# Down tiles by halves of the channels, two first tiles interleaved, zero products and moved sums in a two-layer decoder trunk

## The chip, the core and the metric

The kernel is one program on one core of a Trainium2 chip. The metric is the device time of one execution in microseconds (us): the median of several runs. TensorE is the engine for matrix products (PE, and PEld for its weight loads), VectorE (DVE) and ScalarE (ACT) do the elementwise work, SyncE (SP) issues most transfers.

## What is computed

Two decoder layers over 256 tokens of 1024 channels, all in float32:

```python
for i in range(DEPTH):
    mod = c_act @ w_mod[i] + b_mod[i]
    sh1, sc1, g1, sh2, sc2, g2 = jnp.split(mod, N_MOD, axis=-1)
    h = modulate(rmsnorm(x, norm1_g[i]), sh1, sc1)
    y = short_conv_mixer(...) if i % 2 == 0 else pool_mixer(...)
    x = x + g1[:, None, :] * y
    h = modulate(rmsnorm(x, norm2_g[i]), sh2, sc2)
    x = x + g2[:, None, :] * peer_ffn(h, ...)
return rmsnorm(x, final_g)
```

`peer_ffn` projects `h` to queries, scores them against two sets of 128 keys, picks 16 of 16384 experts for each head and token, and sums `gate * gelu(h . u_expert) * v_expert`. The kernel computes it densely: all experts' products with `u` ("up"), the gates scattered into a dense matrix, and the product with `v` ("down").

## The kernel before, in words

**Tiles.** Every weight matrix is cut into tiles of 128 x 1024. They pass through a ring of 4 slots in one order for the whole program: `conv_in` (24 tiles), `conv_out` (8), `query` (16), `up` (128), `down` (128) in layer 0, then `pool_in` (8), `pool_group` (4), `pool_out` (8), `query`, `up` and `down` again in layer 1. For each tile SyncE loads `raw[s]`, ScalarE rounds it into `high[s]` (L371), VectorE forms the rest `low[s]` (L557, called through `slot`, which works 3 tiles ahead of TensorE), and TensorE multiplies. Each product is made of three: `high` by `mov_h`, `high` by `mov_l`, `low` by `mov_h`, where `mov_h` and `mov_l` are the rounded activations and their rest. The counter `product` goes up by one for each finished tile and frees its slot.

**Projection tiles** (L1093, functions `three` and `project`) are 8 channels x 3 products of 256 columns, into one of the two banks of `ps`. The next tile but one needs the bank emptied (`evac_dve` or `evac_act`).

**Down tiles** (L1242, `down_tile`) are the experts' rows: for each of four banks of `acc` (two halves of the tokens times two halves of the channels; banks 0 and 1 hold the first half of the channels) three products of 512 columns. All 128 tiles add up in the same four banks. Behind the last tile ScalarE (banks 0 and 2, L540) and VectorE (1 and 3, L1026) copy them to `E`; TensorE turns `E` back channel by channel with products by the unit matrix (L1271, eight for each half), `turned_back(c)` lying in `ps` for channels 0 to 3 and in `acc` for 4 to 7; VectorE adds each channel, scaled, to `X` (L1032) and counts `x_ready`.

**Norms.** ScalarE squares each channel of `X` (L400), TensorE adds the squares of each token by products with one column of ones (L1064, two for each channel), ScalarE takes the root (L404), VectorE the reciprocal and a diagonal (L607, L610), TensorE spreads it over the partitions (`spread`, L1080), VectorE scales each channel (`scaled`, L629), ScalarE shifts and rounds it to `mov_h` (L417), VectorE forms `mov_l` (`rest`, L635). In `norm`, `scaled` and `rest` take turns with a lag of two channels. The first tile behind a norm waits for `mov_l` channel by channel (`moving`). There are five norms: 0 and 1 in layer 0, 2 and 3 in layer 1, and the last one, 4. Norms 1 and 3 get their squares already added over the channels (`total`, L683), so that TensorE has only two products there.

**Modulation.** The products of `c` and `w_mod` are formed on VectorE (L576) into `macc`; TensorE adds them over the partitions with products of one column (`sum_mod`, L1053, 8 for each of six parts). For layer 1 parts 0 and 1 are summed right before the last down tile of layer 0. The rows of the experts picked are turned by six products with the unit matrix (L1213, once in each layer).

The order on each engine is that of its program. The engines are tied by semaphores alone.

## Time and profile before

| | |
|---|---|
| median of 3 runs | 1914.95 us (1914.13 to 1916.62) |
| the profiled execution | 1915.88 us, of which 1914.1 us from its first to its last instruction |
| TensorE busy | 1864.7 us (97% of the span) |
| VectorE busy | 1525.1 us (80%) |
| ScalarE busy | 860.3 us (45%) |
| mean granted clock of TensorE | 0.985 of full speed |

The times of single steps below come from that one execution. A busy share of 97% says that nearly all of the time is dense products; the rest sits where TensorE waits or runs at the lower of its two clock levels (1.2 instead of 2.4 GHz, granted clock 0.50). A row's idle time names what ended the wait.

### The profile page before, as it was taken

What the parts mean: (1) busy time and instruction counts of PE and PEld (TensorE: products, weight loads), DVE (VectorE), ACT (ScalarE), POOL (GpSimd) and SP (SyncE); (2) the same over time, 40 slices, a digit from 0 to 9 for tenths busy, and PEclk for the clock granted to TensorE, in tenths of its full rate; (3) what the DMA queues carried; (4) which work ended last, traced back from release to release, by engine and by line L of the source; (5) the groups of instructions that cost most, each with busy time, mean ns of one, the idle gap of its engine ahead of it and who ended that gap; (6) DMA issues with size and microseconds to landing.
All of it is one profiled execution on the core that took longest, in us unless ns stands there. A gap on an engine that the chain in (4) does not pass through costs nothing.

```text
span 1914.1 us, 39829 instructions
## 1 busy us (share of the span) xinstructions
PE 1864.7 (97%) x14820; PEld 1729.5 (90%) x14820; DVE 1525.1 (80%) x2634; ACT 860.3 (45%) x1281; POOL 4.0 (0%) x8
## 2 busy tenths in 40 slices
PE   5989999999999999999999999999999999999998
PEld 5989999999999888888889899999999988888887
DVE  7986698888888888788868668889788888885554
ACT  3334444454334444454544544444433444444543
POOL 0000000000000000000000000000000000000000
PEclk9998999999999999999989999999999999999998
DMA  7976455555454555698835655555445455555552
GB/s 298 333 280 227 145 185 179 185 169 167 159 159 142 170 175 170 235 333 318 316 112 168 243 168 172 183 186 180 164 151 163 138 172 164 174 194 191 191 192 88
DMA packets 101339, 370.38 MB, mean 194 GB/s; under 512 B 11168, under 2 KB 11552, under 8 KB 100640
## 3 DMA queue, kind: packets, MB, share of 16 engines
q1 hardware_dynamic: 100848, 367.43, 57.0%
q10 hardware_dynamic: 432, 2.23, 0.3%
q8 instruction: 29, 0.48, 0.1%
q14 instruction: 30, 0.25, 0.0%
HBM read 366.47 MB, written 3.15 MB: 193 GB/s over the span
## 4 chain that ended last, share of the span: by engine, by line
PE 91%; DVE 6%; DMA 2%; issue 1%; ACT 1%; SPq 0%; DVEq 0%; ACTq 0%
PE ps L1093 46%; PE acc L1242 37%; PE gp L1191 5%; DVE acts L576 2%; DVE low L557 1%; PE gp L1053 1%; PE gp L1180 1%; DMA raw<-conv_in 1%; DMA acts<-w_mod 1%; PE gp L1064 0%; DVE acts L629 0%; DMA raw<-conv_out 0%; DVE acts L934 0%; ACT high L371 0%; PE gp L1080 0%
## 5 line engine op out<-in xcount | busy, mean ns | idle before, releaser
L557 DVE TENSOR_TENSOR low<-raw,high 128x1024 fp32r<-128x1024 f32 x596 | 727.6, 1222 | 325.9 <-ACT high L371 323.6
L371 ACT ACTIVATE high<-raw 128x1024 fp32r<-128x1024 f32 x593 | 626.9, 1057 | 483.4 <-PE acc L1242 384.8
L1093 PE MATMUL ps<-mov_h,high 128*128 128x256 f32 x2704 | 778.8, 288 | 15.2 <-DVE mov_l L635 7.2
L1093 PE MATMUL ps<-mov_l,high 128*128 128x256 f32 x2704 | 770.3, 285 | 0.0
L1093 PE MATMUL ps<-mov_h,low 128*128 128x256 f32 x2704 | 770.0, 285 | 0.0
L1093 PEld LDWEIGHTS ps<-mov_h,high 128*128 128x128 f32 x2704 | 523.7, 194 | 18.7 <-issue 13.9
L1093 PEld LDWEIGHTS ps<-mov_l,high 128*128 128x128 f32 x2704 | 524.8, 194 | 0.0
L1093 PEld LDWEIGHTS ps<-mov_h,low 128*128 128x128 f32 x2704 | 524.2, 194 | 0.0
L1242 PE MATMUL acc<-high,mov_h 128*128 128x512 f32 x1024 | 403.4, 394 | 1.0 <-DVE mov_l L991 0.8
L1242 PE MATMUL acc<-high,mov_l 128*128 128x512 f32 x1024 | 399.6, 390 | 0.0
L1242 PE MATMUL acc<-low,mov_h 128*128 128x512 f32 x1024 | 399.5, 390 | 0.0
L482 ACT ACTIVATE acts<-ps 128x256 f32 (+1 forms) x256 | 98.5, 385 | 433.6 <-PE ps L1093 433.6
L1242 PEld LDWEIGHTS acc<-high,mov_h 128*128 128x128 f32 x1024 | 192.8, 188 | 41.2 <-DVE mov_l L991 2.2
L1242 PEld LDWEIGHTS acc<-high,mov_l 128*128 128x128 f32 x1024 | 192.8, 188 | 40.9
L1242 PEld LDWEIGHTS acc<-low,mov_h 128*128 128x128 f32 x1024 | 193.0, 188 | 39.2
L861 DVE TENSOR_TENSOR hot<-hot,gate 128x1536 bf16<-128x1536 bf16 x128 | 121.9, 952 | 0.0
L576 DVE SCALAR_TENSOR_TENSOR acts<-acts,cact 128x1024 f32<-128x1024 f32 x86 | 110.1, 1280 | 5.8 <-DMA acts<-w_mod 5.4
L991 DVE TENSOR_TENSOR mov_l<-acts,mov_h 128x256 fp32r<-128x256 f32 x256 | 106.5, 419 | 2.7 <-ACT mov_h L514 2.7
L1191 PEld LDWEIGHTS gp<-hot 128*128 128x128 bf16 x3072 | 96.4, 97 | 9.7 <-issue 8.4
L1191 PE MATMUL gp<-hot 128*128 128x64 bf16 x3072 | 104.1, 193 | 0.0
L514 ACT ACTIVATE mov_h<-acts 128x256 fp32r (+1 forms) x256 | 101.4, 399 | 0.0
L857 DVE TENSOR_TENSOR hot<-sm,idx 128x1024 bf16<-128x1024 bf16 x128 | 87.7, 685 | 0.0
(108 smaller groups left out, 743.1 us busy)
## 6 DMA issues: line engine op xcount, KB each, us to landing
raw<-up SPq DMA_DIRECT2D x256, 512.0 KB, 3.3
raw<-down SPq DMA_DIRECT2D x256, 512.0 KB, 3.9
acts<-w_mod SPq DMA_DIRECT2D x84, 512.0 KB, 5.3
raw<-query SPq DMA_DIRECT2D x32, 512.0 KB, 3.5
raw<-conv_in SPq DMA_DIRECT2D x24, 512.0 KB, 6.9
acts<-w_mod SPq DMA_DIRECT2D x6, 1024.0 KB, 15.4
raw<-conv_out SPq DMA_DIRECT2D x8, 512.0 KB, 7.3
raw<-pool_in SPq DMA_DIRECT2D x8, 512.0 KB, 4.4
```

The source lines that it names most:

```text
L371: nc.scalar.activation(flat(high[s]), tile_row(s), ACT.Copy).then_inc(high_ready, 1)
L482: nc.scalar.activation(A[:, bass.ds(i * (RING * T) + (first + s) * T, T)], ps[:, s % 2, 0:T], ACT.Gelu).then_inc(evac_act, 1)
L514: nc.scalar.activation(mov_h[:, s], A[:, bass.ds(g * T, T)] if not isinstance(g, int) else A[:, g * T:(g + 1) * T], ACT.Copy).then_inc(wh_ ...
L557: nc.vector.tensor_tensor(flat(low[n % RING]), tile_row(n % RING), flat(high[n % RING]).bitcast(F32), ALU.subtract).then_inc(low_ready, 1)
L576: return nc.vector.scalar_tensor_tensor(macc[:, m], tile, c, macc[:, m], ALU.mult, ALU.add)
L857: nc.vector.tensor_tensor(hot2[:, u], number(0, P), over(idx2, P), ALU.is_equal)
L861: nc.vector.tensor_tensor(hot1[:, u].rearrange("p h n e two -> p (h n) e two"), eq.unsqueeze(2).broadcast_to([P, PAIRS, PARTS, HALF, 2]).r ...
L991: nc.vector.tensor_tensor(mov_l[:, s], A[:, g * T:(g + 1) * T], mov_h[:, s].bitcast(F32), ALU.subtract).then_inc(wl_ready, 1)
L1053: ins = nc.tensor.matmul(gp[:, 1, m * DC + c:m * DC + c + 1], macc[:, m, c * P:(c + 1) * P], ones[:, 0:1], start=True, stop=True)
L1093: ins = nc.tensor.matmul(dst, w[s][:, c], m[:, mv], start=(first and n == 0), stop=(last and n == 2), skip_group_check=skip)
L1191: ins = nc.tensor.matmul(gp[:, u, j * HALF:(j + 1) * HALF], hot2[:, u, j // 2, :, j % 2], hot1[:, u, j // 2, n, :, j % 2], start=(n == 0), ...
L1242: ins = nc.tensor.matmul(acc[:, b, :], w[:, s, tok], flat(v[s])[:, cols], start=False, stop=(closing and n == 2), skip_group_check=True)
```

## The change

1. **Down by halves.** The last four down tiles of each layer are multiplied for banks 0 and 1 first, all four, then for banks 2 and 3. Between the second halves of the first and the second of them stand the turning back of channels 0 to 3, so that the copies, the additions to `X` and the squares of that half can run beside products. The sums of squares of channels 0 and 1 stand before the turning back of channels 4 to 7. ScalarE and VectorE follow the same order, and the high and low parts of the next layer's first three tiles stand between them.
2. **Two tiles side by side.** `first_two` takes the place of the first two tiles of `pool_in` and of both `query` runs: all products by `mov_h` of both tiles channel by channel, then those by `mov_l`. In `norm`, all eight `scaled` stand before the eight `rest` for norms 1 to 3.
3. **Zeros.** `keep_warm` multiplies 128 x 128 zeros, 12 times before `spread` of norms 1 to 4 and 13 times behind it for norms 1 to 3, into `acc[:, 3]`.
4. **Sums moved.** The two modulation sums of layer 1 stand behind the third and the fourth tile of the second last group of four down tiles, 8 products each; VectorE takes them up behind its last additions to `X`.
5. Turning uses the transpose form of the product instead of a plain product with the unit matrix, 22 of them in each layer.
6. The first four tiles of each loop of projection tiles are written out instead of being the loop's first turn.

```diff
@@ -528,17 +529,31 @@
                     last = n0 + first + HALF - RING
                     if half == 1:
                         load_table(ACT.Sqrt)
-                    for s in range(RING):
-                        if last + s + AHEAD < TILES:
+                    ahead(0, last, 0)
+                    weight(first + HALF - 1, RING - 1)
+                    if half == 0:
+                        for s in range(1, RING):
                             ahead(0, last, s)
-                        if s + AHEAD < RING:
...
+                def evac(b):
                     act.wait_ge(acc_done, 3 * layer + b + 1)
                     nc.scalar.activation(E[:, b % 2, (b // 2) * 512:(b // 2 + 1) * 512], acc[:, b, :], ACT.Copy
                                          ).then_inc(acc_out_act, 1)
+                def squares(c0):
+                    for c in range(c0, c0 + DC // 2):
+                        act.wait_ge(x_ready, layer * DC + c + 1)
+                        square(c)
+                evac(0)
+                squares(0)
+                if layer == 0:
+                    ahead(0, last, 1)
+                    ahead(0, last, 2)
+                evac(2)
+                if layer == 0:
+                    ahead(0, last, 3)
+                squares(DC // 2)
...
-                lag = 4 if shift_last else 2
-                for c in range(DC):
-                    if shift_last and c == lag:
-                        shift_last()
-                    scaled(c)
-                    if k < 4 and c >= lag:
-                        rest(c - lag)
-                if k < 4:
+                if k == 0:
+                    lag = 4
+                    for c in range(DC):
+                        if c == lag:
+                            shift_last()
+                        scaled(c)
+                        if c >= lag:
+                            rest(c - lag)
                     for c in range(DC - lag, DC):
                         rest(c)
-                if k == 0:
                     for n in range(1, AHEAD):
                         rest_of(n)
+                else:
+                    for c in range(DC):
+                        scaled(c)
+                    if k < 4:
+                        for c in range(DC):
+                            rest(c)
...
-                    dve.wait_ge(x_ready, DC)
-                    finish_mod(1, (0, 1))
...
-                for j in range(HALF):
+                for j in range(HALF - AHEAD):
...
-                for b in (1, 3):
-                    if b == 1:
-                        dve.wait_ge(acc_done, 3 * layer + 2)
-                    else:
-                        dve.wait_ge(product, n0 + KEYS + RING)
+                def evac(b):
                     nc.vector.tensor_copy(E[:, b % 2, (b // 2) * 512:(b // 2 + 1) * 512], acc[:, b, :]
                                           ).then_inc(acc_out_dve, 1)
+                def add_to_x(c0):
+                    for c in range(c0, c0 + DC // 2):
+                        if c % 2 == 0:
+                            dve.wait_ge(back, (layer * DC + c) // 2 + 1)
+                        nc.vector.scalar_tensor_tensor(X[:, c], turned_back(c),
+                                                       mod[:, 5 * DC + c:5 * DC + c + 1], X[:, c],
+                                                       ALU.mult, ALU.add).then_inc(x_ready, 1)
+                dve.wait_ge(acc_done, 3 * layer + 2)
+                evac(1)
                 dve.wait_ge(reloaded, 16 * (layer + 1))
-                for c in range(DC):
-                    if c % 2 == 0:
-                        dve.wait_ge(back, (layer * DC + c) // 2 + 1)
-                    nc.vector.scalar_tensor_tensor(X[:, c], turned_back(c),
-                                                   mod[:, 5 * DC + c:5 * DC + c + 1], X[:, c],
-                                                   ALU.mult, ALU.add).then_inc(x_ready, 1)
+                add_to_x(0)
+                slot(n0 + KEYS - 3)
+                slot(n0 + KEYS - 2)
+                dve.wait_ge(product, n0 + KEYS + RING)
+                evac(3)
+                add_to_x(DC // 2)
+                slot(n0 + KEYS - 1)
+                if layer == 0:
+                    finish_mod(1, (0, 1))
+                dve.wait_ge(x_ready, DC * (layer + 1))
...
+            def keep_warm(n):
+                for _ in range(n):
+                    nc.tensor.matmul(acc[:, 3, 0:P], zeros[:], zeros[:], start=True, stop=True)
...
+            def first_two(layer, name, evac, evac0):
+                pe.wait_ge(low_ready, AT[layer, name] + 2)
+                pe.wait_ge(evac, evac0 + 2)
+                def one(s, w, m, c, first, last):
+                    return nc.tensor.matmul(ps[:, s, 0:T], w[s][:, c], m[:, c], start=first, stop=last)
+                for c in range(DC):
+                    pe.wait_ge(mh_done, moved[0] * DC + c + 1)
+                    for s in range(2):
+                        one(s, high, mov_h, c, c == 0, False)
+                        one(s, low, mov_h, c, False, False)
+                lag = DC // 2
+                for c in range(DC + lag):
+                    if c < DC:
+                        moving(c)
+                        ins = one(0, high, mov_l, c, False, c == DC - 1)
+                        if c == DC - 1:
+                            ins.then_inc(product, 1)
+                    if c >= lag:
+                        ins = one(1, high, mov_l, c - lag, False, c - lag == DC - 1)
+                ins.then_inc(product, 1)
...
+            def run_behind_norm(layer, name, tiles, evac, evac0):
+                first_two(layer, name, evac, evac0)
+                for s in range(2, RING):
+                    project(layer, name, 0, s, evac, evac0)
+                with pe.Fori(0, tiles // RING - 1) as i:
...
                 spread(2 * layer)
+                if layer == 1:
+                    keep_warm(13)
...
-                    run(1, "pool_in", 8, evac_dve, 32)
+                    run_behind_norm(1, "pool_in", 8, evac_dve, 32)
...
+                keep_warm(12)
                 spread(2 * layer + 1)
-                run(layer, "query", 16, evac_act, out_act)
+                keep_warm(13)
+                run_behind_norm(layer, "query", 16, evac_act, out_act)
...
-                        ins = nc.tensor.matmul(dst[:, tc * P:(tc + 1) * P], src[:, tc * P:(tc + 1) * P], eye,
-                                               start=True, stop=True)
+                        ins = nc.tensor.transpose(dst[:, tc * P:(tc + 1) * P], src[:, tc * P:(tc + 1) * P], eye)
...
+                        def next_sum(m):
+                            if layer == 0:
+                                pe.wait_ge(next_used, NEXT + NEXT * (DC - 1) + m + 1)
+                                if m == 0:
+                                    pe.wait_ge(weighted, 2 * SETS)
+                                    pe.wait_ge(mod_taken, sums[0])
+                                    sums[0] += 1
+                                ins = mod_products(m)
+                                if m == 1:
+                                    ins.then_inc(msum_done, 1)
+                        with pe.Fori(0, HALF // RING - 2) as i:
                             for s in range(RING):
-                                down_tile(i, s, False)
+                                down_tile(i, s)
                         for s in range(RING):
-                            if layer == 0 and s == RING - 1:
-                                pe.wait_ge(next_used, NEXT + NEXT * DC)
-                                pe.wait_ge(weighted, 2 * SETS)
-                                sum_mod((0, 1))
-                            down_tile(HALF // RING - 1, s, s == RING - 1)
-                for c in range(DC):
-                    if c % 4 == 0:
-                        pe.wait_ge(acc_out_act, 2 * layer + c // 4 + 1)
-                        pe.wait_ge(acc_out_dve, 2 * layer + c // 4 + 1)
-                    for tc in range(TC):
-                        ins = nc.tensor.matmul(turned_back(c)[:, tc * P:(tc + 1) * P], E[:, tc, c * P:(c + 1) * P],
-                                               eye, start=True, stop=True)
-                    if c % 2:
-                        ins.then_inc(back, 1)
-            square_sums(4)
+                            down_tile(HALF // RING - 2, s)
+                            if s >= 2:
+                                next_sum(s - 2)
+                        for s in range(RING):
+                            arrived(HALF // RING - 1, s)
+                            down_banks(s, (0, 1), s == RING - 1)
+                def turn_back(c0):
+                    pe.wait_ge(acc_out_act, 2 * layer + c0 // 4 + 1)
+                    pe.wait_ge(acc_out_dve, 2 * layer + c0 // 4 + 1)
+                    for c in range(c0, c0 + DC // 2):
+                        for tc in range(TC):
+                            ins = nc.tensor.transpose(turned_back(c)[:, tc * P:(tc + 1) * P],
+                                                      E[:, tc, c * P:(c + 1) * P], eye)
+                        if c % 2:
+                            ins.then_inc(back, 1)
+                for s in range(RING):
+                    down_banks(s, (2, 3), s == RING - 1).then_inc(product, 1)
+                    if s == 0:
+                        turn_back(0)
+                square_sums(2 * layer + 2, 0, 2)
+                turn_back(DC // 2)
+                square_sums(2 * layer + 2, 2, DC)
+                keep_warm(12)
             spread(4)
```

In the rows of the order, a row is one instruction or several of one kind, with its line, operation, output and inputs, size, and what it waits for.

TensorE from the last down product of layer 0 to the sums of squares, before:

```order
L1242 MATMUL acc<-high,mov_l 128x512
L1271 MATMUL ps<-sm,acts 128x128 [waits acc_out_dve,acc_out_act]
L1271 MATMUL ps<-sm,acts 128x128 x7
L1271 MATMUL acc<-sm,acts 128x128 [waits acc_out_dve,acc_out_act]
L1271 MATMUL acc<-sm,acts 128x128 x7
L1064 MATMUL gp<-ones,acts 128x1 [waits sq_done,weighted]
```

and of the changed kernel, from its last down product on:

```order
L1315 MATMUL acc<-high,mov_l 128x512
L1099 MATMUL gp<-ones,acts 128x1 [waits sq_done]
L1099 MATMUL gp<-ones,acts 128x1
L1099 MATMUL gp<-ones,acts 128x1 [waits sq_done]
L1099 MATMUL gp<-ones,acts 128x1
L1366 MATMUL acc<-sm,acts 128x128 [waits acc_out_dve,acc_out_act]
L1366 MATMUL acc<-sm,acts 128x128 x7
```

Only the second eight turns are left behind the last down product; the first eight now stand 18 down products earlier, and two channels' sums come before the wait for the copies of banks 2 and 3.

VectorE at the same place (the copies of `acc`, the additions to `X`, the low parts of `pool_in`), before:

```order
L557 TENSOR_TENSOR low<-raw,high 128x1024 [waits high_ready] x3
L1026 COPY acts<-acc 128x512 [waits acc_done]
L1026 COPY acts<-acc 128x512 [waits product]
L1032 SCALAR_TENSOR_TENSOR acts<-ps,mod,acts 128x256 [waits back,reloaded]
```

and now:

```order
L1040 COPY acts<-acc 128x512 [waits acc_done]
L1047 SCALAR_TENSOR_TENSOR acts<-ps,mod,acts 128x256 [waits back,reloaded]
L1047 SCALAR_TENSOR_TENSOR acts<-ps,mod,acts 128x256
L1047 SCALAR_TENSOR_TENSOR acts<-ps,mod,acts 128x256 [waits back]
L1047 SCALAR_TENSOR_TENSOR acts<-ps,mod,acts 128x256
L572 TENSOR_TENSOR low<-raw,high 128x1024 [waits high_ready] x2
L1040 COPY acts<-acc 128x512 [waits product]
```

The three low parts (L557, now L572) have moved from before both copies to behind them, two of them ahead of the copy of bank 3.

TensorE around the spreading of norm 2 (`gp<-acts,ones`), before:

```order
L1064 MATMUL gp<-ones,acts 128x1
L1080 MATMUL gp<-acts,ones 128x128 [waits diag_done] x2
L1109 UNCONDITIONAL_BRANCH [waits evac_act]
L1109 ISA
L1101 REGISTER_ALU [waits low_ready]
L1093 MATMUL ps<-mov_h,high 128x256 [waits ml_done,evac_dve]
L1093 MATMUL ps<-mov_l,high 128x256
```

and now:

```order
L1099 MATMUL gp<-ones,acts 128x1
L1094 MATMUL acc<-zeros 128x128 x12
L1119 MATMUL gp<-acts,ones 128x128 [waits diag_done] x2
L1094 MATMUL acc<-zeros 128x128 x13
L1135 MATMUL ps<-mov_h,high 128x256 [waits evac_dve,mh_done,low_ready,evac_act]
L1135 MATMUL ps<-mov_h,low 128x256
L1135 MATMUL ps<-mov_h,high 128x256
L1135 MATMUL ps<-mov_h,low 128x256
```

The first product behind the norm no longer waits for `mov_l` (`ml_done`), and 25 products with zeros stand around the spreading.

## Rows read from the trace of the kernel before

**Rows 1.** The page: the chain that ended last, shares of the span by engine.

```profile
PE 91%; DVE 6%; DMA 2%; issue 1%; ACT 1%; SPq 0%; DVEq 0%; ACTq 0%
```

**Rows 2.** The same chain in time: start us, us, what.

```profile
151.69 51.82 PE ps L1093 x408
...
204.41 1.68 PE gp L1053 x16
...
232.56 201.59 PE ps L1093 x1680
...
434.15 1.34 PE gp L1213 x12
...
977.18 4.46 PE gp L1053 x32
...
981.64 5.06 PE acc L1242 x12
...
990.27 3.97 PE gp L1064 x32
...
1070.20 51.67 PE ps L1093 x408
...
1723.80 174.38 PE acc L1242 x768
...
1901.75 4.08 PE gp L1064 x32
```

**Rows 3.** Stretches: length, busy us (instructions) of each engine, granted clock, DMA.

```profile
147.00:156.50 9.50, 6.63 (x26) 5.99 (x27) 7.11 (x20) 4.96 (x10) 0.00 (x0) 0.50 0.20 80
...
977.00:979.40 2.40, 2.40 (x24) 2.38 (x22) 1.04 (x1) 1.06 (x1) 0.00 (x0) 1.00 0.56 186
979.50:986.10 6.60, 6.60 (x22) 5.63 (x22) 0.78 (x2) 0.97 (x2) 0.00 (x0) 0.50 0.26 101
986.50:993.00 6.50, 6.50 (x60) 6.46 (x58) 4.39 (x11) 3.24 (x8) 0.00 (x0) 1.00 0.01 4
993.20:1003.20 10.00, 7.13 (x29) 6.48 (x30) 7.25 (x21) 5.06 (x10) 0.00 (x0) 0.50 0.00 0
...
1064.50:1068.00 3.50, 1.07 (x9) 0.96 (x8) 1.63 (x6) 0.68 (x2) 0.00 (x0) 1.00 1.00 356
1068.30:1074.90 6.60, 4.70 (x19) 4.43 (x20) 6.39 (x16) 4.60 (x9) 0.00 (x0) 0.50 0.21 87
...
1904.50:1914.00 9.50, 2.54 (x11) 2.15 (x10) 3.87 (x11) 0.26 (x1) 0.00 (x0) 0.50 0.32 110
```

**Rows 4.** Timeline of VectorE behind the layer boundary: start us, us, instructions, idle before.

```profile
978.36 1.23 DVE L557 TENSOR_TENSOR low<-raw,high 128x1024 fp32r<-128x1024 f32 x1 [1.49 <-ACT high L371]
...
996.50 1.26 DVE L629 SCALAR_TENSOR_TENSOR acts<-acts,gs,gp 128x256 f32<-128x256 f32 x3 [1.12 <-PE gp L1080]
...
1006.91 0.42 DVE L926 COPY acts<-ps 128x256 f32<-128x256 f32 x1 [0.56 <-PE ps L1093]
```

**Rows 5.** Timeline of ScalarE at the same place.

```profile
988.21 3.42 ACT L400 ACTIVATE acts<-acts 128x256 f32<-128x256 f32 x8 [1.89 <-DVE acts L1032]
...
997.08 1.31 ACT L417 ACTIVATE mov_h<-acts,mod 128x256 fp32r<-128x256 f32 x3 [2.56 <-DVE acts L629]
```

**Rows 6.** Timeline of TensorE at the same place.

```profile
995.16 1.22 PE L1080 MATMUL gp<-acts,ones 128*128 128x128 f32 x4 [0.94 <-DVE acts L610]
998.31 0.55 PE L1093 MATMUL ps<-mov_h,high 128*128 128x256 f32 x1 [1.92 <-DVE mov_l L635]
```

**Rows 7.** Timeline of TensorE before the second norm of layer 1.

```profile
1067.56 0.71 PE L1080 MATMUL gp<-acts,ones 128*128 128x128 f32 x4 [0.88 <-DVE acts L610]
```

**Rows 8.** Timeline of TensorE: zero products before the first down tile.

```profile
603.90 1.07 PE L1231 MATMUL acc<-zeros 128*128 128x128 bf16 x16
```

**Rows 9.** Timeline of VectorE at the end of layer 1.

```profile
1898.21 0.69 DVE L1026 COPY acts<-acc 128x512 f32<-128x512 f32 x1 [0.67 <-PE acc L1242]
1899.17 1.70 DVE L1032 SCALAR_TENSOR_TENSOR acts<-ps,mod,acts 128x256 f32<-128x256 f32 x4 [0.27 <-PE ps L1271]
```

89 lines of the change are left out of this document (47 added, 42 removed).

## Prediction, made before the changed kernel ran

> **What bounds the kernel now.** The chain that ended last comes first: 91% of it is TensorE [rows 1], and read in time it is nearly all dense stretches, so elementwise work moved beside them costs nothing. The products stay the same in number; a gain must come from the gaps, from the low clock, or from cheaper small products. I then read the stretches around each gap, for busy time and granted clock, and the timelines inside them for who waits for whom. The unit prices are: a projection tile is 201.59 / 70 = 2.88 us; a down tile 174.38 / 64 = 2.72, half of one 1.36 [rows 2]. Five places are left: the norm before `query` in either layer, the layer boundary, the end, and the turning of the rows picked.
>
> **The clock.** It stands at 2.4 GHz (1.00) in dense work and at 1.2 GHz (0.50) for 9.5 us from 147.0, 6.6 from 979.5, 10 from 993.2, 6.6 from 1068.3 and from 1904.5 to the end [rows 3]. Before each fall TensorE had full-width products, then only one-column products or idled: it fell 2.3 us after the sums began at 977.2, and some 2.8 us after the sums began at 990.3 [rows 2, 3]. Before 1068 it had idled since about 1064.4, 3.8 us. I take 3.1 us from the last full product to the fall. It came back 4.9 us (998.31 to 1003.2) and 4.7 us (1070.2 to 1074.9) after full products resumed [rows 2, 3, 6]; I take 4.9. A single run of eight one-column sums of 1.68 us between tiles never brought it down [rows 2].
>
> **Norm before `query`, layer 0.** Nothing ahead of the fall at about 146.6 changes. Before, the first tile waits for VectorE, which takes two steps of 0.40 us a channel (`scaled`, `rest`), and starts 1.81 us behind the first `scaled` (996.50 to 998.31 in the like norm [rows 4, 6]). Here the stretch from 151.69 holds 17 tiles [rows 2]: 16 at 2.88 leave 5.8 us for the first, so the second ends at 160.4. Now only `mov_h` is waited for, in steps of 0.40 (three in 1.31 us, the first 0.58 behind `scaled` [rows 4, 5]), so TensorE starts 1.2 us behind it. At the high clock it needs 4 x 0.12 = 0.48 a channel, ends `mov_h` at 5.0, then 16 `mov_l` products; VectorE ends its 16 steps at 6.4, which holds the last, and both tiles are done 7.2 us behind the first `scaled`, against 10.4. The gain would be 3.2. The zeros: 16 take 1.07 us, so 0.057 each at the high clock, and I take twice that at the low [rows 8]. Twelve last 0.7 or 1.3 us, where the wait for the diagonal is 0.9 [rows 6]; at the low clock they push the spread back 0.35. But TensorE then has full-width products from 147.6, so the clock returns at 152.5, 1 us into the first two tiles, and the rest is held by `mov_l` anyway. With 0.35 and some 0.7 of this lost I take **2.1** (0.7 if zeros do nothing for the clock, 3.5 if it never falls).
>
> **Norm before `query`, layer 1.** The zeros start at 1066.7, before the fall at 1068.2; the clock would be back at 1071.6 instead of 1075.0, and twelve at the high clock fit. First product at 1070.2, 17 tiles in 51.67 [rows 2], second tile done at 1078.7. Now 7.2 to 7.8 behind the first `scaled` at 1068.4, and a wait of ScalarE for the bank, some 0.2. **2.4** (1.0 to 3.1).
>
> **Turning the rows picked.** Six plain products took 1.34 us, 0.22 each [rows 2], on the chain in each layer. No row shows the transpose form. Bounds: 0.22, no change, and 0.057, what a single pass of 128 columns takes [rows 8]. I take 0.11, since one of the 8 sums of 1.68 us also costs two passes of 0.105 that only the weight load can fill [rows 2]. 2 x 6 x 0.11 = **1.3** (0 to 2.0).
>
> **Layer boundary.** Before, the sums at 977.18 take 4.46 us, and the last tile 5.06, because the clock fell in them [rows 2, 3]. Split, each is 1.68 and the tiles 2.72. From 966.1 (the start of the fourth last but one tile, four tiles ahead of 977): sum 1.68, tile 2.72, sum 1.68, so the last group starts at 972.2; the first halves end at 977.6, one second half at 979.0, the turning (0.9) at 979.9, three second halves at 984.0. The first copies (0.69 [rows 9]), four additions (1.70 [rows 9]) and four squares (3.42 / 2 [rows 5]) fit beside that: free, and their cover is 4.1 us of products. Not free: ScalarE's squares put the roundings of `pool_in` late, VectorE stands behind them with two low parts of 1.23 [rows 4] and copies bank 3 at 985.4 instead of 984.2. So that queue costs 1.2 us, of which two channels' sums fill 0.8. Copy 0.7, turning 0.9, additions and squares close behind: at the high clock the last sum would end at 989.6, against 994.2 before (990.27 + 3.97). But the last full product is at 984.0, so the clock falls at about 987.1; six channels' sums at 0.84 instead of 0.42 then end near 992.1. The twelve zeros (1.3), the spread at the low clock (1.22, against 0.71 [rows 6, 7]) put the first `scaled` at 994.7, against 996.50: 1.8. Behind it the copy of the second tile decides, since VectorE runs without a pause after it: it ended 10.8 us behind `scaled` [rows 4]; now two low parts (2.5) and two copies (0.84) follow the 16 steps, 9.6. **3.0** in all (0.7 with an early fall; 6.5 with none).
>
> **The end.** The same without low parts or sums to move: last product at 1898.9, copy to 1899.8, turning to 1900.7, last sum at 1903.2 or, with a fall at 1902.0, at 1904.5, against 1905.8 [rows 2]. Zeros at the low clock delay the spread 0.35: **0.95** (-0.3 to 2.5).
>
> **Sum.** 2.1 + 2.4 + 1.3 + 3.0 + 0.95 = 9.75 us, from 1915.88 to 1906.1. The profiled run is 0.9 above the median of three, so **1905.2**.
>
> **A rule against it.** The turns before (16 records in 1.8 us, twice, at 986.5 to 990.3) ran at granted clock 1.00, and it held until 993.0 [rows 3]. The Trainium skill, TensorE: Matmul & The Clock Gate (Part 4: PE-mode transpose) says that the transpose form doesn't count as activity for the clock and gives about 275 ns for one in a kernel. By 275 ns, an estimate from that page, 44 turns would cost 2.4 us more than plain ones, not 4.8 less. No run here shows either yet; the first half is rival two.
>
> **Rivals.** *One: the clock never falls.* If zeros and turns hold it at all places, the upper ends hold in the norms and most of the others: 3.5 + 3.1 + 1.3 + 5 + 2 = 15 us, 1900. Against it: the gap of the boundary is 5 us without a full product. *Two: neither turns nor zeros count.* The clock falls at 986 and 1900.8 and returns 4.9 us after the first two tiles start: 0.7 + 1.0 + 1.3 + 0.7 - 0.3 = 3.4, 1911.5. *Three: TensorE's program.* It grows from 2901 to 3446 rows, written out at nine places (a loop's first four tiles, the two first tiles, the last group); if code had to be fetched at each and TensorE stood 1.1 us, the gain of 9.75 is gone, and at 2 us it is 1914.95 + 8 = 1923. Against it: unrolled and looped tiles run at 2.88 without a gap through 201.59 us [rows 2]. *Four: the split starves TensorE.* Half tiles come every 1.36 us. The last high part waits for the tile before the group, 1.06 us of ScalarE, then 1.2 and 0.4 of VectorE, 2.9 in all against 3 x 1.36 = 4.1. It costs nothing until 1.2 us more are lost.
>
> **How the numbers follow.** Forecast 0.65, one 0.11, two 0.17, three and four together 0.04, the rest (turns as dear as before, 1907.8) 0.03. The likeliest case spans 1902 to 1909; with rival one and part of two the range is 1899.5 to 1910.5. A measurement tells 0.2%, 3.8 us, from no change: below 1911.1 lies all but half of two and the slower cases. Faster 0.89, same 0.08, slower 0.03.
>
> **What would show it.** Six turns in about 0.66 us. Two separate sums of 1.68 at 966 with clock 1.00, and a last group without a gap of over 0.2. Second tile of `query` done 2 to 3 us earlier after either norm. Zeros at 0.057 or 0.107, and the low stretches cut from 9.5 and 6.6 to about 6 and 3.5 us. Sums of the last norm ending near 1904.5 less what was gained before. I am wrong if the clock stays low into the third tile, if bank 3's copy is later than 1.5 us behind the last product, or if gaps appear where the program was written out.

## The result, and the profile after

The changed kernel takes 1901.1 us (1899.17 to 1903.38, median of 4), beside 1914.97 (1914.13 to 1916.62) of the kernel before on the same chip: a ratio of 0.9929 with an interval of 0.9914 to 0.9943. The profiled execution is one of 1903.38 us with a span of 1901.6, so it is compared with the 1915.88 and 1914.1 of before: 12.5 us less in both.

The page of the changed kernel: busy time of the engines; the DMA queue of the instructions (packets, MB, share of the engines); the chain by engine.

```profile
PE 1860.2 (98%) x14863; PEld 1726.2 (91%) x14863; DVE 1524.4 (80%) x2634; ACT 858.2 (45%) x1281; POOL 4.0 (0%) x8
...
q8 instruction: 34, 0.56, 0.1%
...
PE 91%; DVE 5%; DMA 2%; issue 1%; ACT 1%; SPq 0%; DVEq 0%; ACTq 0%
```

TensorE still has 91% of the chain, as in [rows 1]. The chain in time (start us, us, what), with the same pieces as [rows 2]:

```profile
150.49 6.14 PE ps L1135 x48
...
229.19 201.59 PE ps L1156 x1680
...
431.44 11.50 PE ps L1156 x96
...
962.15 1.68 PE gp L1077 x16
963.83 2.89 PE acc L1315 x12
966.71 1.68 PE gp L1077 x16
968.39 6.97 PE acc L1315 x30
...
983.18 4.69 PE gp L1099 x24
...
1062.99 6.19 PE ps L1135 x48
...
1891.14 2.59 PE gp L1099 x24
```

The two first tiles of `query` now stand as a piece of their own, 48 products in 6.14 and 6.19 us. The two modulation sums are two pieces of 1.68, where one of 4.46 stood, and the last six sums of the last norm take 2.59, where eight took 4.08 [rows 2]. The loops of 70 tiles are still 201.59, and the six turns behind the first of them leave 0.66 (229.19 + 201.59 ends at 430.78, the next piece starts at 431.44) where 1.34 stood.

Stretches of the changed kernel: length, busy us (instructions) of PE, PEld, DVE, ACT, POOL, granted clock, DMA share, GB/s.

```profile
147.00:150.40 3.40, 3.40 (x29) 3.06 (x26) 1.90 (x7) 0.84 (x3) 0.00 (x0) 0.51 0.64 265
150.60:156.00 5.40, 5.40 (x44) 5.30 (x45) 5.02 (x14) 5.05 (x10) 0.00 (x0) 1.00 0.00 0
983.40:993.40 10.00, 10.00 (x60) 9.74 (x60) 6.20 (x19) 4.33 (x12) 0.00 (x0) 0.50 0.30 96
1060.00:1070.00 10.00, 9.11 (x84) 8.51 (x83) 8.34 (x21) 7.38 (x15) 0.00 (x0) 1.00 0.25 103
1889.00:1894.60 5.60, 5.32 (x53) 5.05 (x52) 2.80 (x8) 2.01 (x6) 0.00 (x0) 1.00 0.01 3
1894.80:1901.00 6.20, 1.08 (x4) 0.79 (x4) 3.23 (x9) 0.00 (x0) 0.00 (x0) 0.50 0.45 169
```

Against [rows 3]: the low stretch of layer 0's norm is 3.4 us and not 9.5 long; the one at 1068 is gone; the one of 6.6 at the modulation sums is gone; that behind the boundary is still 10; and at the end the clock holds until all sums are done.

To place every microsecond, the span is cut at events that all kernels here have. **A** ends at VectorE's reciprocal of norm 1, **B** at the end of the 17th tile behind it, **C** at the start of the second half of the down tiles of layer 0, **D** at its last down product, **E** at the reciprocal of norm 2, **F** at the reciprocal of norm 3, **G** at the end of the 17th tile behind it, **H** at the second half of layer 1's down tiles, **I** at its last down product, **J** at the end. us, of one profiled execution each.

| kernel | span | A | B | C | D | E | F | G | H | I | J |
|---|---|---|---|---|---|---|---|---|---|---|---|
| before | 1914.1 | 148.01 | 55.50 | 601.97 | 181.06 | 8.08 | 72.40 | 54.85 | 601.93 | 174.22 | 16.08 |
| changed | 1901.6 | 147.34 | 52.80 | 601.23 | 178.80 | 8.12 | 72.10 | 52.31 | 601.23 | 175.12 | 12.55 |
| after_again | 1897.1 | 145.02 | 52.83 | 601.24 | 178.81 | 6.00 | 71.15 | 52.96 | 601.22 | 175.11 | 12.76 |
| no_zeros | 1902.2 | 145.06 | 54.05 | 601.27 | 178.84 | 6.31 | 73.47 | 54.41 | 601.27 | 175.15 | 12.37 |
| plain_turns | 1900.5 | 144.30 | 52.81 | 601.97 | 179.75 | 6.55 | 70.43 | 52.81 | 601.95 | 176.06 | 13.87 |
| slots_late | 1900.9 | 146.70 | 52.81 | 601.24 | 178.84 | 6.94 | 71.57 | 52.81 | 601.27 | 175.15 | 13.57 |
| sums_together | 1903.2 | 146.02 | 53.09 | 601.23 | 181.95 | 7.30 | 71.22 | 53.00 | 601.23 | 175.11 | 13.05 |
| no_halves | 1912.7 | 147.80 | 53.66 | 601.24 | 177.91 | 14.18 | 72.73 | 52.98 | 601.23 | 174.21 | 16.76 |
| one_by_one | 1905.1 | 145.67 | 55.13 | 601.23 | 178.81 | 7.89 | 72.99 | 54.85 | 601.24 | 175.10 | 12.19 |
| tail_zeros | 1898.2 | 146.13 | 52.81 | 601.24 | 178.80 | 6.00 | 71.27 | 52.93 | 601.28 | 175.10 | 12.64 |
| before_zeros | 1912.4 | 146.67 | 55.13 | 601.94 | 179.20 | 7.83 | 73.82 | 54.89 | 601.95 | 174.23 | 16.74 |
| before_side | 1905.7 | 145.38 | 53.84 | 601.95 | 179.21 | 7.83 | 70.98 | 54.29 | 601.93 | 174.22 | 16.07 |
| halves_alone | 1907.6 | 145.90 | 55.66 | 601.94 | 179.71 | 6.55 | 71.99 | 54.90 | 601.93 | 176.01 | 13.01 |
| one_slot | 1900.0 | 146.40 | 52.90 | 601.24 | 178.81 | 6.23 | 71.57 | 52.81 | 601.27 | 175.15 | 13.62 |

Changed less before, read from the first two rows: norm of layer 0 (B) 2.70, norm of layer 1 (G) 2.54, turning of the picked rows (C and H) 0.74 and 0.70, boundary (D, E, F) 2.26 - 0.04 + 0.30 = 2.52, end (I, J) 3.53 - 0.90 = 2.63, and A 0.67: 12.5 in all.

### The profile page after: what moved, and what is told of

It reads as the page before. It is cut to its first block, busy times and chain, and to the rows that moved or that the text cites. A ratio compares the mean times of both kernels' runs of the same rounds, so it can differ in the third digit from the quotient of the medians.

```text
span 1901.6 us, 39850 instructions
## 1 busy us (share of the span) xinstructions
PE 1860.2 (98%) x14863; PEld 1726.2 (91%) x14863; DVE 1524.4 (80%) x2634; ACT 858.2 (45%) x1281; POOL 4.0 (0%) x8
## 4 chain that ended last, share of the span: by engine, by line
PE 91%; DVE 5%; DMA 2%; issue 1%; ACT 1%; SPq 0%; DVEq 0%; ACTq 0%
PE ps L1156 46%; PE acc L1315 36%; PE gp L1267 5%; DVE acts L591 2%; DVE low L572 2%; PE ps L1135 1%; PE gp L1077 1%; DMA raw<-conv_in 1%; PE gp L1256 1%; DMA acts<-w_mod 1%; PE gp L1099 0%; ACT high L371 0%; DMA raw<-conv_out 0%; PE acc L1094 0%; DVE acts L952 0%
## 5 line engine op out<-in xcount | busy, mean ns | idle before, releaser
L572 DVE TENSOR_TENSOR low<-raw,high 128x1024 fp32r<-128x1024 f32 x596 | 727.7, 1222 | 320.6 <-ACT high L371 318.5
L1156 PE MATMUL ps<-mov_h,high 128*128 128x256 f32 x2656 | 761.2, 287 | 9.9 <-DVE mov_l L680 5.4
L1156 PE MATMUL ps<-mov_l,high 128*128 128x256 f32 x2656 | 755.4, 284 | 0.0
L1156 PE MATMUL ps<-mov_h,low 128*128 128x256 f32 x2656 | 755.2, 284 | 0.0
L1156 PEld LDWEIGHTS ps<-mov_h,high 128*128 128x128 f32 x2656 | 513.4, 193 | 11.5 <-issue 8.2
L1156 PEld LDWEIGHTS ps<-mov_l,high 128*128 128x128 f32 x2656 | 513.7, 193 | 0.0
L1156 PEld LDWEIGHTS ps<-mov_h,low 128*128 128x128 f32 x2656 | 513.6, 193 | 0.0
```

The lines of the kernel that those rows point to most:

```text
L572: nc.vector.tensor_tensor(flat(low[n % RING]), tile_row(n % RING), flat(high[n % RING]).bitcast(F32), ALU.subtract).then_inc(low_ready, 1)
L1156: ins = nc.tensor.matmul(dst, w[s][:, c], m[:, mv], start=(first and n == 0), stop=(last and n == 2), skip_group_check=skip)
```

## The experiments

Theory: the gain is a sum of four things that TensorE feels at the places where it waits, and half or more of it is clock. Rivals: single parts are worth nothing and one does the work; or the parts help each other, so that neither taking one out nor putting one in alone gives its share. Each kernel is one edit of the changed kernel, or one part of it alone on the kernel before. Medians are of 5 to 12 executions; the kernels were run in three groups of four, each group on one chip with the kernel before beside it (medians 1913.2, 1914.15, 1914.0). Differences to the changed kernel are taken from its median in the first group, 1901.1; sums_together, no_halves and one_by_one ran in the second, where the kernel before took 1.0 more, so what they cost may be up to 1.0 less than is said. What a part costs in the pieces is read against the row after_again, unless another is named.

### The changed kernel again

No edit.

> The changed kernel as it is, once more, as the base for the others of this group. Theory one (the low stretches of TensorE's clock decide what is left to chance): the time lies in 1899 to 1903.5 us again, and the low stretches lie elsewhere in the norms than in the first profile (there 147.1 to 150.3, 983.2 to 993.5, none in the second norm of layer 1, 1894.7 to the end); a run with later falls is faster. Rival (the spread of 4 us comes from the transfers or the host): the low stretches are the same to 0.5 us and the times spread all the same.

1901.1 us (1898.65 to 1902.55), ratio 0.994 (0.9927 to 0.9954). Its profiled execution is 4.5 us shorter than the first one, though it is the same program: A is 2.32 less, E 2.12 less. TensorE at its boundary, and the clock:

```profile
977.90 0.95 PE L1099 MATMUL gp<-ones,acts 128*128 128x1 f32 x8
...
980.73 2.74 PE L1099 MATMUL gp<-ones,acts 128*128 128x1 f32 x24
...
980.00:984.20 4.20, 4.16 (x44) 3.99 (x43) 3.20 (x9) 1.86 (x5) 0.00 (x0) 1.00 0.56 192
984.50:987.50 3.00, 3.00 (x19) 2.74 (x20) 1.88 (x7) 1.15 (x3) 0.00 (x0) 0.50 0.49 165
```

The 24 sums take 2.74 us here and 4.85 in the first profile (below), because the clock fell 6.4 us and not 3.1 us behind the last down product. So E swings by 2 us from one execution to the next, and A, of which the change touches only the first tiles of `conv_in`, by 3.7: 144.30 to 148.01 over the fourteen rows. C, D, H and I repeat within 0.06 us wherever the program is the same, but for D in before (181.06, and 179.20 in before_zeros and before_side). B and G repeat within 0.2, but for B in sums_together and no_halves (53.09, 53.66), where the clock was low for 6.8 us and not 3.4, and G in the first profile (52.31). F, which holds `pool_in` to `pool_out`, goes with the low stretches too: 72.10 in the first profile, 71.15 here.

### Zero products

```diff
             def keep_warm(n):
-                for _ in range(n):
-                    nc.tensor.matmul(acc[:, 3, 0:P], zeros[:], zeros[:], start=True, stop=True)
+                pass
```

> Only the zero products are taken out (25 at each of norms 1 to 3, 12 at norm 4); nothing else is left out. Theory one (full-width products with zeros hold or bring back the clock): the low stretch at the norm of layer 0 is about 10 us long again instead of 3.2, the one at the second norm of layer 1 is there again (about 7 us), and the time is 2 to 4 us above that of the changed kernel. Rival (the gain in the norms is the order of the two tiles, zeros are idle work): within 0.5 us of the changed kernel, low stretches equally long.

1904.08 us (1902.03 to 1907.36), ratio 0.996 (0.9945 to 0.9975): 3.0 slower than the changed kernel. B is 1.22 longer, G 1.45, F 2.32; E and J stay within what they swing by. The low clock stays for the two tiles of the norm:

```profile
1059.50:1066.00 6.50, 5.12 (x22) 4.85 (x23) 5.38 (x16) 4.53 (x9) 0.00 (x0) 0.50 0.32 134
```

Each piece is one profile, but B and G divide cleanly: in the two kernels with the tiles side by side and without zeros (this one and before_side, below) B is 53.84 and 54.05 and G 54.29 and 54.41, in the eight with both B is 52.80 to 53.66 and G 52.31 to 53.00.

And zeros alone, on the kernel before, at the same places:

> The kernel before with the zero products alone: 12 ahead of the spreading of norms 1 to 4, 13 behind that of norms 1 to 3; tiles one after the other, nothing else changed. Theory A (zeros pay only where TensorE, not VectorE, sets the first tiles): in the kernel without tiles side by side, but with zeros, the stretch from the reciprocal of norm 1 to its 16th tile was 55.13 us against 55.50, the last stretch of norm 3 82.08 against 82.09. So alone they bring 0 to 1 us in all: ratio 0.9995 to 1.000, about 1913.5. Rival B (the clock comes back 3 to 5 us earlier at three norms, and each microsecond at the high clock is worth half of one): 3 x 1.5 = 4.5 us, ratio 0.9977, about 1909.5. Rival C (at the last norm and the boundary zeros at the low clock delay the spreading): 0.3 to 0.7 us slower.

1913.32 us (1911.65 to 1918.09), ratio 1.0004 (0.9993 to 1.0015): not told from nothing. Its norm of layer 0:

```profile
146.13 1.44 PE L1060 MATMUL acc<-zeros 128*128 128x128 bf16 x12
...
148.32 1.59 PE L1060 MATMUL acc<-zeros 128*128 128x128 bf16 x13
...
147.00:150.40 3.40, 2.92 (x23) 2.59 (x20) 2.18 (x8) 1.17 (x3) 0.00 (x0) 0.50 0.00 0
150.80:156.00 5.20, 4.48 (x28) 3.45 (x27) 4.24 (x11) 3.96 (x7) 0.00 (x0) 1.00 0.00 0
```

The clock is back at 150.6, as in the changed kernel, but then TensorE has 28 products in 5.20 us where it could do 43: the one first tile follows VectorE's two steps a channel whatever the clock. B is 55.13 against 55.50, G 54.89 against 54.85. A clock that comes back earlier is worth something only where TensorE's work, not VectorE's, sets the end of the piece.

### Tiles side by side

```diff
+                        if k < 4 and c >= 2:
+                            rest(c - 2)
                     if k < 4:
-                        for c in range(DC):
+                        for c in range(DC - 2, DC):
                             rest(c)
...
-                first_two(layer, name, evac, evac0)
-                for s in range(2, RING):
+                for s in range(RING):
```

> Only the interleaving of the first two tiles is undone, with the old turn-taking of scaled and rest on VectorE for norms 1 to 3; the zeros stay. Theory: three norms lose the 2 to 3 us that waiting for mov_l channel by channel costs (first tile 5.8 to 6.3 us instead of two tiles in 6.2): +2 each in the two query norms and +0.5 to +1.5 at the layer boundary, where VectorE bounds what follows: 4.5 to 6 us slower. Rival (with the clock kept high by zeros the single tile would be as fast): under 1.5 us.

1907.14 us (1904.15 to 1908.62), ratio 0.9968 (0.9956 to 0.998): 6.0 slower than the changed kernel. B is 55.13 and G 54.85, what they are with zeros alone: 2.3 and 1.9 us are gone, and F is 1.84 longer. Alone on the kernel before (`first_two` for the first two tiles of `pool_in` and both `query` runs, `scaled` ahead of `rest` in norms 1 to 3):

> The kernel before with the two tiles side by side alone: all scaled ahead of rest in norms 1 to 3, the first two tiles interleaved at pool_in and both query runs. Theory A (parts overlap: without zeros the two tiles run at the low clock): norm 1 gains 1.4 (the kernel without zeros had 54.05 against 55.50), norm 3 0.5 (81.66 against 82.09), the boundary about 1.5: 3.4 us, ratio 0.9982, about 1910.7. Rival B (parts add: taking the two tiles out of the changed kernel cost 6.0 us, so they bring 6.0 here): ratio 0.9969, about 1908.1.

1910.52 us (1907.1 to 1914.96), ratio 0.999 (0.9978 to 1.0002): 3.5 on the medians, but the interval holds 1. B is 1.66 shorter and G 0.56. TensorE in its norm of layer 0:

```profile
148.48 0.55 PE L1101 MATMUL ps<-mov_h,high 128*128 128x256 f32 x1 [1.34 <-ACT mov_h L417]
...
144.80:151.00 6.20, 3.91 (x17) 3.56 (x18) 4.46 (x14) 3.43 (x9) 0.00 (x0) 0.50 0.41 172
```

Products of 256 columns come every 0.21 us here, until 151.3, and every 0.12 behind; 48 of them take 7.24 us against 6.14. So the two parts carry each other. Alone they bring 0.37 + 1.66 = 2.03 in B and -0.04 + 0.56 = 0.52 in G; together 2.67 and 1.89 (after_again). Side by side, TensorE has enough work to be the bound, and then the clock counts.

### Halves of the channels

```diff
-                            down_banks(s, (0, 1), s == RING - 1)
+                            down_banks(s, range(4), s == RING - 1).then_inc(product, 1)
...
-                for s in range(RING):
-                    down_banks(s, (2, 3), s == RING - 1).then_inc(product, 1)
-                    if s == 0:
-                        turn_back(0)
+                turn_back(0)
```

> Only the halving is undone: each of the last four down tiles does its four banks in one go, both groups of eight turns stand behind the last product, all else as in the changed kernel (also VectorE's two low parts ahead of the copy of bank 3). Theory one (halving takes the first turns, four additions and four squares off the tail): from the last down product to the last sum of squares 1.5 to 2.5 us more at the end of layer 1 and 2 to 4 more at the layer boundary, in all 3 to 6 us slower than the changed kernel. Rival (the sums of squares bound the tail, 32 records of 0.105 to 0.2 us, whatever stands before them): under 1.5 us in all.

1910.78 us (1908.29 to 1914.53), ratio 0.9986 (0.9977 to 0.9995): 9.7 slower than the changed kernel. This is not the price of the halves. ScalarE and VectorE keep the changed order here, and it is wrong without halves:

```profile
979.44 0.69 DVE L1040 COPY acts<-acc 128x512 f32<-128x512 f32 x1 [7.44 <-PE acc L1315]
...
984.40 2.36 DVE L572 TENSOR_TENSOR low<-raw,high 128x1024 fp32r<-128x1024 f32 x2 [1.43 <-ACT high L371]
986.68 0.69 DVE L1040 COPY acts<-acc 128x512 f32<-128x512 f32 x1
...
987.51 1.94 PE L1366 MATMUL acc<-sm,acts 128*128 128x128 f32 x8 [4.16 <-DVE acts L1040]
```

The rows are VectorE's timeline, and one of TensorE's. The last product ends at 980.6, but bank 3 is copied at 986.68, behind the additions and two low parts, and TensorE waits 4.16 for it: E is 14.18. At the end of layer 1 the copies of banks 2 and 3 stand behind squares and additions in the same way, and I with J is 3.1 longer. So the halves were put in alone: the changed kernel without zeros, without tiles side by side and with plain turns.

> The changed kernel without zeros, without tiles side by side and with plain turns: left are the down tiles by halves and the two modulation sums apart. Theory A (terms of the prediction as measured): the end 2.6 less 0.5 for plain turns, the boundary 2.5 to 3.5, of it the split sums up to 3.3: 5.5 us, ratio 0.9971, about 1908.5; reciprocal of norm 2 some 185 to 187 us behind the start of the down tiles (189.14 before), norm 1 and norm 3 as before (55.5 and 82.1). Rival B (what taking the halves out cost, 9.7 us): ratio 0.995, about 1904.5. By B the split is worth more than everything else; by A the kernel without halves lost extra by its queue order.

1909.95 us (1907.24 to 1912.06), ratio 0.9983 (0.9974 to 0.9992): 4.1 on the medians. In its profile D is 1.35 shorter than in the first row, E 1.53, F 0.41, and I with J 1.28; B and G are as before (55.66, 54.90). Of the 3.29 in D, E and F the parted sums buy 1 to 3 (next); by this estimate the halves proper bring 1.3 us at the end and 0.1 to 2 at the boundary.

### The two sums apart

```diff
-                            if s >= 2:
-                                next_sum(s - 2)
+                        next_sum(0)
+                        next_sum(1)
```

> Only the two moved modulation sums of layer 1 stand together (3.4 us of one-column products) ahead of the last group of four down tiles instead of one behind each of two tiles. Theory (a run of 1.7 us between tiles is too short to bring the clock down, 3.4 us is not): the clock falls during them or up to 1 us behind them in most executions and the last group runs for some 5 us at 1.2 GHz: +1.5 to +3.5 us between the third and the last group, where the split sums cost 3.4 in all. Rival (where the sums stand doesn't matter, only that the last tile isn't behind them): no low stretch before the last down product, the same time within 0.5 us.

1903.71 us (1901.68 to 1905.07), ratio 0.9948 (0.9934 to 0.9963): 2.6 slower than the changed kernel. Its chain at that place, and its clock:

```profile
963.84 4.68 PE gp L1077 x32
968.52 8.96 PE acc L1315 x30
...
966.00:972.50 6.50, 6.50 (x22) 5.63 (x23) 1.92 (x3) 0.00 (x0) 0.00 (x0) 0.50 0.31 105
```

4.68 + 8.96 stand against 1.68 + 1.68 + 6.97 of the changed kernel: 3.3 us, all clock, and D is 181.95 against 178.80. It fell 2.1 us behind the start of the 16 one-column sums. Where the sums stand together at their old place, it fell 2.4 us behind their start in before and 4.7 behind it in before_zeros and before_side (D is 181.06, 179.20 and 179.20). Against those two the changed kernel's D gains 0.4 and not 2.26, though it holds a turning of 0.9 more; so the parting is worth 1 to 3 us, as the clock happens to fall.

### The form of the turns

```diff
-                        ins = nc.tensor.transpose(dst[:, tc * P:(tc + 1) * P], src[:, tc * P:(tc + 1) * P], eye)
+                        ins = nc.tensor.matmul(dst[:, tc * P:(tc + 1) * P], src[:, tc * P:(tc + 1) * P], eye,
+                                               start=True, stop=True)
```

and the same in `turn_back`.

> Only the 44 turns are plain products with the unit matrix again. If a transpose form costs one weight load of 0.11 us and a plain one two: each group of six 1.34 instead of 0.66 us on the path (+1.36 in all), each eight 1.8 instead of 0.9, the second eight of either layer on the path (+1.8), so 3 us slower in all, less up to 1.5 us where the turns now keep the clock high longer. Rival (the transpose form doesn't count as activity and so costs clock in the tails): the falls behind the last down product come later than 3 us with plain turns, and the total is within 1 us of the changed kernel.

1902.91 us (1902.31 to 1903.76), ratio 0.9952 (0.9938 to 0.9965): 1.8 slower. C and H are as before (601.97, 601.95), D and I 0.95 longer. TensorE at its end:

```profile
1887.66 2.02 PE L1367 MATMUL acc<-sm,acts 128*128 128x128 f32 x16
```

### VectorE's queue at the boundary

```diff
-                slot(n0 + KEYS - 3)
-                slot(n0 + KEYS - 2)
                 dve.wait_ge(product, n0 + KEYS + RING)
                 evac(3)
                 add_to_x(DC // 2)
+                slot(n0 + KEYS - 3)
+                slot(n0 + KEYS - 2)
                 slot(n0 + KEYS - 1)
```

> Only the two low parts of pool_in that VectorE makes ahead of the copy of bank 3 at the layer boundary are moved behind the additions. In the changed kernel they end 0.9 us after the last down product's result was there, and TensorE waits 0.99 us for that copy. Theory one: the copy starts 0.9 us earlier, more of the sums of squares run before the fall of the clock, and the stretch from the last down product to the first scaled channel (10.1 us) is 1 to 2 us shorter. Rival: the low parts are then late for the first pool_in tiles and the gain is given back (same time, wait of TensorE at the first product of pool_in).

1902.31 us (1900.23 to 1902.71), ratio 0.9942 (0.9929 to 0.9956): no gain. The wait of 0.99 for the copy of bank 3 is gone, but the low parts now stand where the norm's reciprocal is wanted. Two kernels more went after the same microsecond: twelve zero products into a free part of `gp` in that wait, ahead of the second `turn_back` of layer 0,

> Only added: 12 zero products in the 1 us in which TensorE waits for the copy of bank 3 at the layer boundary (into a free part of another bank). Theory (full-width products hold the clock): the fall comes more than 4 us behind the last down product instead of 3.1 in the first profile, all the sums of squares run at 2.4 GHz, and the stretch from the last down product to the first scaled channel is 8 us as in the luckier profile (there 977.9 to 985.8) instead of 10.1. Rival (they are too few to count, or what matters is only the moment at which the fall happens to come): the fall still comes about 3 us behind the last product in one of two profiles; time within 0.5 us of the changed kernel.

1900.18 us (1899.91 to 1902.42), ratio 0.9935 (0.992 to 0.9949), and the same with one of the two low parts moved behind the additions:

> The changed kernel with 12 zero products into a free part of gp ahead of the second turning in layer 0, and on VectorE one low part, not two, ahead of the copy of bank 3 (the other behind the additions). Theory A (the copy was 0.30 to 0.99 us late, and the low part behind costs nothing because the second tile of pool_in waits for the last step of the norm anyway): 0.3 to 0.8 us faster than the same kernel with two ahead (1900.2), reciprocal of norm 2 184.2 behind the start of the down tiles, about 1899.6, ratio 0.993. Rival B (given back, as with both moved, where the first copies of pool_in came as much later): 1900.2 to 1901, pool_out no earlier than 43.9 + 184.8 behind the start of down.

1899.51 us (1898.41 to 1901.74), ratio 0.9932 (0.9917 to 0.9946). All three overlap the changed kernel's runs; none is shown to beat it. In tail_zeros the clock fell 6.7 us behind the last down product and E is 6.00, but after_again has 6.4 and 6.00 without these zeros, so that they hold the clock isn't shown. VectorE in one_slot, and then in after_again:

```profile
981.47 1.66 DVE L1047 SCALAR_TENSOR_TENSOR acts<-acc,mod,acts 128x256 f32<-128x256 f32 x4 [1.23 <-PE acc L1366]
983.04 2.35 DVE L572 TENSOR_TENSOR low<-raw,high 128x1024 fp32r<-128x1024 f32 x2
...
985.58 0.17 DVE L622 RECIPROCAL acts<-acts 128x2 f32<-128x2 f32 x1
```

```profile
982.08 1.22 DVE L572 TENSOR_TENSOR low<-raw,high 128x1024 fp32r<-128x1024 f32 x1
...
983.90 0.17 DVE L622 RECIPROCAL acts<-acts 128x2 f32<-128x2 f32 x1 [0.47 <-ACT acts L405]
```

With one more low part behind the additions VectorE runs without a pause into the reciprocal, which is late by it; with two ahead of the copy it waits 0.47 for ScalarE. E is 6.23 with one and 6.94 with both moved, against 6.00. That is within what E swings by, so the rows show where the low part's 1.2 us go, and not what it costs.

### Parts and sum

| part | taken out costs | alone brings |
|---|---|---|
| zeros | 3.0 | 0.7 (not told from 0) |
| side by side | 6.0 | 3.5 (the interval just holds 0) |
| halves | 9.7, part of it an order that doesn't fit | 4.1 with the sums apart |
| sums apart | 2.6 | |
| turns | 1.8 | 1.4 (C and H, profile) |
| together | 23.1 | 9.7 |

The whole brings 12.1 to 13.9 on the medians. So the parts alone fall short of it by 2 to 4 us, which isn't clear of the noise, since each of the three medians is good to some 2 us; taken out one at a time they exceed it by far. The last rival holds: for B and G its mechanism is shown above, and for the halves it is the order of the queues.

## Why the prediction was right, and where it wasn't

Predicted were 1905.2 us, 1899.5 to 1910.5; measured 1901.1. The direction and the range hold, and the mechanism of each part in the main; what was set too firmly is when the clock falls and comes back. Of the 4.1 us between forecast and median 2.75 come from the terms below and from A (12.5 against 9.75). The other 1.35 are luck: the profiled execution of the changed kernel lies 2.3 above its median, where that of before lay 0.9 above. By its own steps:

**Norm of layer 0: 2.1, measured 2.70.** The two tiles are done 7.4 us behind the first `scaled` (149.22 to 156.6), where 7.2 was worked out. The zeros began at 146.80 and the clock was back at 150.5, 3.7 us later; I had taken 4.9 and 152.5. Over the ten kernels with zeros that was 2.8 to 6.0 us, and B brought 1.8 to 2.7 in the eight that have both parts, so 2.70 is the upper end. The spreading at the low clock wasn't later than before either: the first `scaled` is 1.88 us behind the reciprocal in both profiles. Of the 1.05 us written off for these two, 0.5 were lost.

**Norm of layer 1: 2.4, measured 2.54**, with the clock at 1.00 from 1060 to 1070. Here too the tiles end 7.4 behind `scaled`. This was partly luck: in the other executions with zeros and side by side it was low for 3.4 us at that place, and G was 0.5 to 0.7 more.

**Turning the picked rows: 1.3, measured 0.74 + 0.70.** TensorE's row reads

```profile
430.62 0.82 PE L1289 MATMUL gp<-sm,acts 128*128 128x128 f32 x6
```

and six turns at 0.11 are the 0.66 that the prediction named.

**Boundary: 3.0, measured 2.52.** TensorE and VectorE of the changed kernel:

```profile
980.17 0.95 PE L1099 MATMUL gp<-ones,acts 128*128 128x1 f32 x8
982.11 1.07 PE L1366 MATMUL acc<-sm,acts 128*128 128x128 f32 x8 [0.99 <-DVE acts L1040]
983.01 4.85 PE L1099 MATMUL gp<-ones,acts 128*128 128x1 f32 x24
987.73 1.44 PE L1094 MATMUL acc<-zeros 128*128 128x128 bf16 x12
...
981.28 0.68 DVE L1040 COPY acts<-acc 128x512 f32<-128x512 f32 x1
...
990.24 3.22 DVE L644 SCALAR_TENSOR_TENSOR acts<-acts,gs,gp 128x256 f32<-128x256 f32 x8 [1.19 <-PE gp L1119]
```

From the first sum (962.15) to the last down product there are 18.0 us, as worked out (17.9). Bank 3 is copied 1.1 behind the product (1.4), the clock falls 3.1 behind (3.1), the sums end 7.7 behind (8.1), `scaled` starts 10.1 behind (10.7). So 2.15 was won up to `scaled`, where 1.8 stood. What didn't hold in this execution is the step behind it, that the second tile's copy ends 9.6 instead of 10.8 us behind `scaled` and carries the 1.2 us on: it ended 10.2 behind, and from `scaled` to the start of `pool_out` only 0.37 are left (42.91 against 43.28). ScalarE, then VectorE:

```profile
997.82 2.01 ACT L371 ACTIVATE high<-raw 128x1024 fp32r<-128x1024 f32 x2 [2.75 <-PE ps L1135]
...
998.91 1.23 DVE L572 TENSOR_TENSOR low<-raw,high 128x1024 fp32r<-128x1024 f32 x1 [0.54 <-ACT high L371]
1000.06 0.42 DVE L944 COPY acts<-ps 128x256 f32<-128x256 f32 x1
```

TensorE ran the two tiles at the low clock until 993.5, 3.3 us behind the first `scaled`; ScalarE's next high part waits for the first of them, and VectorE 0.54 for that part. In after_again, plain_turns and sums_together the clock was high from 1.9 us behind `scaled` at the latest. There the copy ended 9.6 behind it, and `pool_out` started 41.8 to 42.0 behind it, so the 1.2 us came through. What the step left out is the clock. In the changed kernel's first profile TensorE also waits 1.8 us at 1006.3 for a copy of VectorE, where before had two such waits of 0.9 together:

```profile
PE ps L1156 <- DVE acts L944: 1.8, 1, 1.8
```

Columns: who waits for whom, us in total, times, longest. With the later fall of after_again the boundary as a whole (D, E and F) brings 261.54 - 255.96 = 5.58, inside the 0.7 to 6.5 that the prediction gave.

**The end: 0.95, measured 2.63.** This is the term that was mis-sized.

```profile
1889.04 0.95 PE L1099 MATMUL gp<-ones,acts 128*128 128x1 f32 x8
1890.08 1.06 PE L1366 MATMUL acc<-sm,acts 128*128 128x128 f32 x8
1890.98 2.74 PE L1099 MATMUL gp<-ones,acts 128*128 128x1 f32 x24
1893.58 0.83 PE L1094 MATMUL acc<-zeros 128*128 128x128 bf16 x12
1894.66 1.22 PE L1119 MATMUL gp<-acts,ones 128*128 128x128 f32 x4 [0.25 <-DVE acts L625]
```

The last sum ends 4.7 us behind the last down product, and 4.3 was worked out for a clock that doesn't fall and 5.6 for one that does; it then fell at 1894.7, 5.6 us behind, and not at 3.1. The failed step is the one value of 3.1 us from the last full product to the fall. Over the twelve profiled executions after the first it was 3.3 to 8.1 us where it fell at all. The trace of before had warned: its last down product ended at 1898.2 and the clock fell at 1904.5 [rows 2, 3], 6.3 us later. I had counted the plain turns in between as full work, which is open to doubt, and gave one value where the runs show a spread of 5 us. The zeros of this norm cost the spreading nothing (0.83 us at the high clock, then a wait of 0.25), where 0.35 was set. Another 0.47 of the 2.63 are chance: from the first `scaled` to the end it took 6.15 us in before and 5.68 here, but 5.67 in before_side too, whose program is that of before at this place.

**The rest.** 0.67 us of the 12.5 lie in A, which swings by more than that. *Rival one* (the clock never falls) held in the first profile only in layer 1's norm, and in plain_turns up to `scaled` at the boundary. *Rival two* (neither zeros nor turns count) is wrong for the zeros at the norms: behind the reciprocal of norm 1 the clock was back after 2.3 to 5.4 us in the ten kernels with zeros and after 5.9 to 9.2 in the four without. At the boundary they aren't shown to do anything for it: it was low for anything from nothing to 13.7 us with them, and for 10.2 in no_zeros. *Rival three* (fetching the program) is wrong: the queue of instructions moved 0.56 MB (0.48 before), no gap stands where the tiles are written out, and 70 tiles still take 201.59 us. *Rival four* (the split starves TensorE) is wrong: 30 products stand in 6.97 us without a gap, and D repeats to 0.04 us.

## What to carry over

Behind a norm, first ask which engine ends the piece: zeros that bring the clock back were worth nothing that could be told from noise where VectorE did, and 3.0 us where two tiles side by side had made TensorE the bound. Taking a part out of a kernel whose other queues were ordered for it measures the misfit too, so put the part in alone as well. And one profile places a gain, but with a clock that falls 3 to 8 us behind the last dense work it doesn't size it.
